# A finer start for the first products: weight quarters, a shared rounding, and another order of the first transfers in a one-core mLSTM/GLA trunk step

## The reference, cut to what matters

```python
def rmsnorm(x, g):
    y = x32 * lax.rsqrt(jnp.mean(x32 * x32, axis=-1, keepdims=True) + EPS)
    return (y * g.astype(jnp.float32)).astype(x.dtype)

a = rmsnorm(h, W['norm_mix_g'][i])
z = a @ W['w_in'][i]        # columns mq, mk, mv, mi, mf, mo, gq, gk, gv, glr, gg, ga, gb
```

## Time and profile before

| | us |
|---|---|
| median of 3 runs | 1179.3 (1179.1 to 1180.03) |
| the profiled execution, its own time | 1179.56 |
| its span, first to last instruction | 1177.8 |
| TensorE busy | 1166.9 |
| VectorE busy | 757.5 |
| ScalarE busy | 393.0 |

### The profile page before, as it was taken

One profiled execution on the slowest core, in us unless ns is written; L12 is line 12 of the kernel. 1 busy time (PEld: TensorE's weight loads), 2 busy tenths in 40 slices (PEclk: granted clock), 3 DMA queues, 4 the chain that ended last, 5 costly groups with the idle time before them and its releaser, 6 DMA issues.

```text
span 1177.8 us, 21827 instructions
## 1 busy us (share of the span) xinstructions
PE 1166.9 (99%) x9177; PEld 1110.2 (94%) x9177; DVE 757.5 (64%) x1396; ACT 393.0 (33%) x577; POOL 2.3 (0%) x7
## 2 busy tenths in 40 slices
PE   9999999999999999999999999999999999999997
PEld 8999999999999999999999999999999999999996
DVE  6855568675777655664664667777777764333678
ACT  6243232133443322333333223323333321112544
POOL 0000000000000000000000000000000000000000
PEclk9999999999999999999999999999999999999998
DMA  6342232422313366554443542122122133222232
GB/s 221 113 146 88 93 108 90 144 73 93 113 68 109 122 226 225 179 175 143 148 141 130 179 148 72 72 87 93 72 85 95 62 119 133 91 92 97 72 108 82
DMA packets 48962, 138.56 MB, mean 118 GB/s; under 512 B 5460, under 2 KB 25108, under 8 KB 39776
## 3 DMA queue, kind: packets, MB, share of 16 engines
q1 hardware_dynamic: 16392, 89.39, 21.8%
q10 hardware_dynamic: 32472, 47.77, 11.9%
HBM read 113.15 MB, written 23.81 MB: 116 GB/s over the span
## 4 chain that ended last, share of the span: by engine, by line
PE 94%; issue 2%; DVE 2%; ACT 1%; DMA 1%; ACTq 0%; POOL 0%; POOLq 0%; DVEq 0%
PE ps L782 33%; PE ps L810 10%; PE ps L808 6%; PE ps L811 6%; PE ps L809 6%; PE ps L911 6%; PE ps L788 6%; PE ps L812 5%; PE ps L917 3%; PE ps L829 2%; PE aux L1074 1%; DMA xT<-in_xT 1%; PE aux L1138 1%; PE aux L1034 1%; PE aux L1062 1%
## 5 line engine op out<-in xcount | busy, mean ns | idle before, releaser
L782 PE MATMUL ps<-apair,whi 128*128 128x288 f32 x1728 | 275.1, 298 | 0.6 <-ACT mq L2090 0.5
L782 PEld LDWEIGHTS ps<-apair,whi 128*128 128x128 f32 x1728 | 243.4, 189 | 4.8 <-issue 2.0
L1189 DVE TENSOR_TENSOR wlo<-wraw,whi 128x2048 fp32r<-128x2048 f32 (+1 forms) x82 | 176.1, 2147 | 74.8 <-ACT whi L1935 70.5
L1935 ACT ACTIVATE whi<-wraw 128x2048 fp32r<-128x2048 f32 (+1 forms) x87 | 156.4, 1797 | 106.9 <-PE ps L812 52.5
L810 PE MATMUL ps<-apair,whi 128*128 128x512 f32 x336 | 132.1, 393 | 0.0
L808 PE MATMUL ps<-apair,whi 128*128 128x320 f32 x336 | 105.0, 313 | 0.0
L811 PE MATMUL ps<-apair,wlo 128*128 128x320 f32 x336 | 104.2, 310 | 0.0
L809 PE MATMUL ps<-apair,whi 128*128 128x320 f32 x336 | 103.8, 309 | 0.0
L782 PE MATMUL ps<-apair,wlo 128*128 128x288 f32 x448 | 96.0, 296 | 0.0
L812 PE MATMUL ps<-apair,wlo 128*128 128x256 f32 x336 | 95.1, 283 | 0.0
L812 PEld LDWEIGHTS ps<-apair,wlo 128*128 128x128 f32 x336 | 63.2, 188 | 14.2
(11 more groups left out here) (415 smaller groups left out, 2090.6 us busy)
## 6 DMA issues: line engine op xcount, KB each, us to landing
wraw<-in_w_in SPq DMA_DIRECT2D x31, 1024.0 KB, 4.9
wraw<-in_w_up SPq DMA_DIRECT2D x21, 1024.0 KB, 4.9
gate_scratch<-stg ACTq DMA_DIRECT2D x32, 288.0 KB, 3.0
gt<-gate_scratch ACTq DMA_DIRECT2D x32, 288.0 KB, 2.9
wraw<-in_w_pgate SPq DMA_DIRECT2D x6, 1024.0 KB, 4.7
wraw<-in_w_down SPq DMA_DIRECT2D x8, 704.0 KB, 4.1
wraw<-in_w_down SPq DMA_DIRECT2D x8, 640.0 KB, 3.8
out_C_s<-st ACTq DMA_DIRECT2D x16, 256.0 KB, 3.0
```

What stands on the lines that cost most here:

```text
L782: mm = nc.tensor.matmul(ps[:, t % 2, a, 0:HALF], w, x(k)[:, a * HALF:(a + 1) * HALF], start=f, stop=e)
L1189: V.tensor_tensor(wlo[:, s, 0:n], wraw[:, s, 0:n], f32(whi[:, s, 0:n]), ALU.subtract)\
L1935: A.activation(whi[:, s, 0:n], wraw[:, s, 0:n], ACT.Copy).then_inc(split_hi, 1)
```

## The change

- SP: the first half of unit 0's weights is issued as two quarters, k = 0 to 1 and k = 2 to 3, each with its own semaphore. SP then waits until the first quarter has landed before it issues the second half and misc.
- ScalarE: only the first two token pieces are issued ahead of the dummy Sqrt with its table load, the other three behind it.
- VectorE rounds the first quarter itself, as its first work in `norm_in`; ScalarE rounds only the second quarter, behind ahi 1 instead of behind ahi 0. The low part of the first half is formed in two quarters, behind alo 0 and alo 1.
- TensorE waits for the second quarter at k = 2 (`hi_second`, `lo_first` at 2), and within a block k it takes both output blocks with ahi before it waits for alo.

```diff
             return x[:, k - k0, :]
 
+        def quarter(q):
+
+            return slice(q * UW // 4, (q + 1) * UW // 4)
+
...
                 if u == 0:
-                    sp.dma_start(wraw[:, 0, 0:UW // 2], ins["w_in"][0, :, 0:UW // 2]).then_inc(raw_first, 16)
+                    sp.dma_start(wraw[:, 0, quarter(0)], ins["w_in"][0, :, quarter(0)]).then_inc(raw_first[0], 16)
+                    sp.dma_start(wraw[:, 0, quarter(1)], ins["w_in"][0, :, quarter(1)]).then_inc(raw_first[1], 16)
+                    sp.wait_ge(raw_first[0], 16)
                     sp.dma_start(wraw[:, 0, UW // 2:], ins["w_in"][0, :, UW // 2:]).then_inc(raw_in[0], 16)
                     sp.dma_start(misc_raw[:, :, :], ins["w_misc"]).then_inc(misc_in, 16)
...
                     if k == 0:
                         pe.wait_ge(hi_first, 1)
+                    elif k == 2:
+                        pe.wait_ge(hi_second, 1)
                     elif k == KT // 2:
                         pe.wait_ge(split_hi, 1)
                         pe.wait_ge(split_lo, 1)
-                    pe.wait_ge(a_hi, k + 1)
-                    pe.wait_ge(a_lo, k + 1)
-                    for n in range(2):
-                        col = (2 * k + n) * P
-                        for x in (ahi, alo):
+                    for x, ready in ((ahi, a_hi), (alo, a_lo)):
+                        pe.wait_ge(ready, k + 1)
+                        for n in range(2):
+                            col = (2 * k + n) * P
                             for a in range(2):
                                 nc.tensor.matmul(ps[:, t + n, a, 0:HALF], whi[:, 0, col:col + P],
                                                  x[:, k, a * HALF:(a + 1) * HALF],
                                                  start=k == 0 and x is ahi, stop=False)
-                    if k == 0:
-                        pe.wait_ge(lo_first, 1)
+                    if k in (0, 2):
+                        pe.wait_ge(lo_first, k // 2 + 1)
...
                 if s[0] == "norm_in":
+                    dve.wait_ge(raw_first[0], 16)
+                    V.tensor_copy(whi[:, 0, quarter(0)], wraw[:, 0, quarter(0)]).then_inc(hi_first, 1)
                     dve.wait_ge(gains_in, 16)
...
-                        if k == 0:
-                            dve.wait_ge(hi_first, 1)
-                            V.tensor_tensor(wlo[:, 0, 0:UW // 2], wraw[:, 0, 0:UW // 2], f32(whi[:, 0, 0:UW // 2]),
+                        if k < 2:
+                            dve.wait_ge((hi_first, hi_second)[k], 1)
+                            V.tensor_tensor(wlo[:, 0, quarter(k)], wraw[:, 0, quarter(k)], f32(whi[:, 0, quarter(k)]),
                                             ALU.subtract).then_inc(lo_first, 1)
...
-            for n, (k0, k1) in enumerate(X_PIECES):
+            for n, (k0, k1) in enumerate(X_PIECES[:2]):
                 act.dma_start(xT[:, k0:k1, :], ins["xT"][:, k0:k1, :]).then_inc(x_in[n], 16)
             act.wait_ge(init_done, 1)
             A.activation(stat[:, 0, :], stat[:, 1, :], ACT.Sqrt).then_inc(act_warm, 1)
+            for n, (k0, k1) in enumerate(X_PIECES[2:]):
+                act.dma_start(xT[:, k0:k1, :], ins["xT"][:, k0:k1, :]).then_inc(x_in[n + 2], 16)
             act.wait_ge(act_warm, 1)
...
-                            if k == 0:
-                                act.wait_ge(raw_first, 16)
-                                A.activation(whi[:, 0, 0:UW // 2], wraw[:, 0, 0:UW // 2], ACT.Copy).then_inc(hi_first, 1)
+                            if k == 1:
+                                act.wait_ge(raw_first[1], 16)
+                                A.activation(whi[:, 0, quarter(1)], wraw[:, 0, quarter(1)], ACT.Copy).then_inc(hi_second, 1)
```

More of the change, by code:

```diff
@@ L436, in build @@
         raw_in = sems("raw_in", 2)
-        raw_first = sem("raw_first")
+        raw_first = sems("raw_first", 2)
         hi_first = sem("hi_first")
+        hi_second = sem("hi_second")
         lo_first = sem("lo_first")
```

## The result

| | before | after |
|---|---|---|
| median of 7 runs, us | 1179.35 (1179.1 to 1180.03) | 1182.39 (1181.98 to 1184.01) |
| ratio, with its 95% interval | | 1.0029 (1.0019 to 1.0039) |
| the profiled execution | 1179.56 | 1182.06 |
| its span | 1177.8 | 1180.2 |
| unit 1 starts on TensorE at | 23.89 | 26.18 |

The account below looks back on a forecast made before the run. TensorE, busy 99%, bounds the kernel, with 1.6 us reachable in the opening. Its line gains 0.69 + 0.47 = 1.2 us, the ScalarE and VectorE line 1.2: median 1178.1 us, range 1177.7 - 0.3 to 1179.3 + 0.3.

Parts of the forecast that it names:

- The two lines that set unit 1's start: Opening: TensorE's products, and beside them the loads, ScalarE and VectorE up to mq's copy; both must come 1.2 us earlier.
- the table load not held by init_done: ScalarE's opening: the load might run from 1.7 or, held, from 2.5; the sum stays either way; no chance given.
- With quarters the SP packet is 2 KB: SP's queue, 3 to 5 us: 47% of an unchanged 0.60 MB, so quarter 0 lands near 4.8.
- the second line: Token piece 2, second weight half, ScalarE and VectorE in turn, mq copied: 1.2 us earlier, mq copied at 22.55.
- TensorE's own line: TensorE through unit 0 and misc: 0.69 + 0.47 = 1.2 us earlier, misc products ending at 22.3.
- k = 0 then takes 1.61, not 2.08: 0.47 us go: TensorE, first step of unit 0: hidden waits vanish because alo 0 and low weights are done by 7.7 at worst.
- the second half has its 0.52 MB complete 1.7 us later, at 9.7: SP's second weight half, behind the wait: lands at 9.7, the wait costs it 0.2 us, rounding from about 9.8.
- Rival C: Second half behind SP's wait needs 7.8 us again, lands at 12.7, rounding 1.7 us later; 1181.0 us; 6%.
- The rule of the Trainium skill: Second half's transfer: 2.0 us plus bytes at 436 GB/s, some 3.2 us, landing near 8.2; the prediction trusted the trace instead.
- Rival A: Second half comes as if nearly alone, landing at 8.4; second line moves 1.56 us; 1177.7 us; 12%.
- The range: Whole kernel: from 1177.7 - 0.3 to 1179.3 + 0.3, covering two rivals with the spread of runs.
- The chance for no change: Whole kernel: effect within about 0.2% (2.4 us), as all 1.6 us in reach are less; 3% each side beyond.

Follow-up runs that it names:

- b2: Changed kernel with the first half of the weights in one transfer and without SP's wait; median 1181.54 us (ratio 1.0014).
- a3: Changed kernel with all five token pieces issued ahead of the table load again, SP's wait kept; 1183.06 us (ratio 1.0031).
- a1: Changed kernel without SP's wait for quarter 0; 1182.59 us (ratio 1.0023).
- a2: Kernel before with one edit: SP waits until the first half has landed before issuing the second half; 1180.55 us (ratio 1.0013).
- b3: Kernel before with SP waiting for the first half, and the last two token pieces placed behind ahi 1; 1181.44 us (ratio 1.0018).
- c1: b2 with 20 warm-up products instead of 15; 1180.34 us (ratio 1.0013).
- a4: Kernel before with only the change's token order, two pieces ahead of the table load and three behind; 1179.35 us (ratio 1.0000).
- d1: Kernel before with unit 1's rounding on ScalarE two squares earlier; 1179.09 us (ratio 0.9998).
- d2: b2 with 17 warm-up products and unit 1's rounding behind the second square; 1179.38 us (ratio 1.0000).

## Why the prediction was wrong

**What held.** The two lines that set unit 1's start, and that the second one decides: unit 1 moved by 2.29 us, the rounding of the second half by 13.29 - 11.01 = 2.28. The first product at 7.27 with 0.16 us of wait, VectorE's copy (0.43 us against 0.44), the table load not held by init_done, token piece 2 earlier (9.0, though not 8.0), unit 1's and the constants' transfers out of the way, nothing later that adds more than 0.1 us to the profiled execution. The warm-up's end held as well (7.11 for 7.17), by luck: the same 15 products ended at 6.04 in b2 and 6.39 in a3. The first product at 7.2 is luck in part too: quarter 0 came 1.9 us later than forecast, and the warm-up hid all but 0.16 us of it.

**The step that failed: "With quarters the SP packet is 2 KB, so it gets 47% of the same 0.60 MB, 0.28 MB: quarter 0 (0.26 MB) lands near 4.8".** I had seen in the earlier trace rows that the queues take turns by packet (96 and 110) and then held the bytes of the stretch fixed, instead of the packets. The runs show the packets all but fixed so early: 80 in the microsecond from 4 to 5 before, 81 after, with 0.26 and 0.17 MB. The earlier trace rows with the count held would have said so: SP's queue moved 240 - 144 = 96 packets from 3 to 5 us, fewer than the 128 of a quarter, so it could not be in near 4.8. The second slip is in the same sentence: it reckons when the bytes have moved on average, and a transfer is in with the last of its 16 parts. From 3 to 5 us SP's queue did move 115 packets and 0.22 MB, most of a quarter, and the first part of quarter 0 was in at 4.34; the last came at 6.69, the landing. For the half before, the last came at 6.73. Inside the change the quarters make the second line 1.35 us later (a1 against b2).

The same step took a part of TensorE's own line. "k = 0 then takes 1.61, not 2.08: 0.47 us go" rested on alo 0 and the low weights "done by 7.7 at worst"; with quarter 0 at 6.69 VectorE rounded it at 6.79 and formed alo 0 only from 7.13 and the low weights until 8.55. k = 0 took 1.97 us (7.27 to 9.24), so TensorE's line gained 0.7 us by k = 1 and not 1.2. b2, with the half in one transfer, has the same 1.97.

**The step that followed: "the second half has its 0.52 MB complete 1.7 us later, at 9.7", its wait costing 0.2 us.** It was issued at 6.71, not 4.9, and then stood 3.3 us without a packet behind the token pieces. I had reckoned turns between the queues from the moment of issue. In after, a2 and b3 the turns begin only when most of what was issued earlier on the other queue has passed. a2 prices the wait by itself, without the quarters: 1.2 us; inside the change it adds 0.77 us to the second line.

**Rival C** named this wait, its place and the row: 7.8 us from issue, decided by a landing past 11.0. The time was 6.6 us from issue. I gave it 6% because "before, the 7.8 us held 0.5 MB of the first half ahead of it"; three token pieces were the like. With quarter 0 at 6.69 and either end of the earlier trace rows, 4.8 or 7.8 us, the landing is 11.5 or 14.5, past the point of decision in both cases; with quarter 0 at 4.9 the lower end gave 9.7, before it. So the first slip is what made C look far. C had the wait and the place right, its 7.8 us were 1.2 too many.

**The rule of the Trainium skill** (DMA: Bandwidth & Descriptors, "Anatomy of one DMA — SWDGE (gpsimd) path"), a fit for transfers that GpSimd issues, would have the half land 3.2 us after its issue, an estimate from that page. The trace, where SP issues, disagrees: 6.6 us here, 7.8 before. Rival A, which has the same consequence from rows, fell with it.

**The range.** Its upper end, 1179.6, left out C. The profiled execution's 2.5 us are the two steps above. The median's 3.0 us are 0.5 more, because before's profiled execution lies 0.2 us above its median and after's 0.3 below: with three of the seven executions in the longer group the median is the highest of the other four. That those three are ones with a low TensorE clock is what a1's and a3's profiles suggest; no profile of the change itself shows it. The prediction had no term for the clock.

**The chance for no change** rested on the sentence that all of the 1.6 us in reach are less than 0.2%. That bounds a gain only. A loss in an opening where one transfer waits for another has no such bound.

## What to carry to other kernels

Where transfers begin a kernel, count packets as well as bytes, and ask when the last part of a transfer is in, not the average one: here cutting a transfer by columns kept one packet a partition, halved what each turn brought, and spread the parts. Be slow to put a transfer behind a wait while another queue has large ones outstanding; in after and a2 it started behind nearly all of them. And before a first product is made earlier, look at what the second unit waits for: here the 0.7 us ahead of the first product were real and recovered to 0.2, and b2 shows that alone they only lengthen a later gap.

## What the runs showed that I had not expected

- From 4 to 5 us after the start both queues together moved 75 to 90 packets in twelve of thirteen kernels, of 2 to 4 KB; from 7 to 9 us the bytes were alike (0.81 to 0.86 MB in all but b3) and the packets were not (213 in after, 251 before, 308 in b2).
- The 16 parts of the first half landed within 0.9 us of each other, those of quarter 0 within 2.4, those of b3's second half within 3.8.
- A transfer on SP's queue, issued at 6.6 to 6.7, had no packet until 9.5 to 10 us while 1.06 MB of token pieces passed on ScalarE's queue in 2.5 us; issued at 6.22 with nothing ahead but one piece, it had packets before 7.5.
- A gap of TensorE of about 1.15 us ahead of unit 1 went with a second group of executions, 1.5 us longer (b2 seven of eleven, c1 five, a2 two); with 0.28 to 0.54 us there (a4, d1, d2) there was none in 33 executions. In a1 the granted clock was 0.50 from 27.0 to 30.4 us, after the gap had ended and in a stretch in which TensorE was busy throughout.
- The end of the warm-up isn't fixed: 15 products ended at 7.17 with the clock record beginning at 6.3, and at 6.04 in b2 with it beginning at 4.0.
